# Two-block layer kernel: row numbers for the second experts by a table in memory

## What is computed

```python
g_star = jnp.argmax(p_group, axis=-1)
e_sel = jnp.take_along_axis(e_logits, g_star[:, None, None], axis=1)[:, 0]
top_v, top_i = lax.top_k(softmax(e_sel), 2)
expert_idx = g_star[:, None] * 4 + top_i
...
a = einsum("nd,edf->nef", h, w_gate)      # D=1024, F=256
b = einsum("nd,edf->nef", h, w_up)
u = silu(a) * b * combine[..., None]      # zero but for the two chosen experts
y = einsum("nef,efd->nd", u, w_down)
```

## Time and profile before

| what | us |
|---|---|
| runs | 1757.52, 1756.31, 1753.81 (median 1756.31) |
| profiled execution | 1755.57 |
| its span, first to last instruction | 1753.8 |
| TensorE busy | 1680.8 (96%) |
| VectorE busy | 723.7 (41%) |
| ScalarE busy | 402.5 (23%) |
| GpSimd busy | 21.9 (1%) |

### The profile page before, as it was taken

How to read it: one execution, slowest core, us unless ns; L and a number is a source line. 1 busy time by engine, 2 the same in 40 slices (tenths; PEclk the granted TensorE clock), 3 DMA queues, 4 the chain that set the end, 5 groups by cost and what they waited for, 6 DMA issues and landing times. The chain is left out here.

```text
span 1753.8 us, 21522 instructions
## 1 busy us (share of the span) xinstructions
PE 1680.8 (96%) x8621; PEld 942.0 (54%) x8621; DVE 723.7 (41%) x1333; ACT 402.5 (23%) x742; POOL 21.9 (1%) x29
## 2 busy tenths in 40 slices
PE   7999999999999999999999999999999998987987
PEld 3576565568876443444344334444488664454543
DVE  4645523667545011011101216975762514451515
ACT  5212113443123110101010031116631023311112
POOL 0000000000000000000000000000000000000001
PEclk9999999999999999999999999999999999999999
DMA  9421276111324999999999960311122131279964
GB/s 363 142 93 48 81 260 235 49 49 48 144 97 191 408 419 427 422 419 421 428 419 420 422 248 27 118 48 49 49 96 77 68 144 72 110 295 376 326 253 180
DMA packets 90287, 374.37 MB, mean 213 GB/s; under 512 B 10381, under 2 KB 11741, under 8 KB 75101
## 3 DMA queue, kind: packets, MB, share of 16 engines
q1 hardware_dynamic: 82652, 350.16, 50.7%
q10 hardware_dynamic: 4496, 12.06, 1.8%
q0 software_dynamic: 3056, 11.01, 1.7%
HBM read 466.53 MB, written 10.49 MB: 272 GB/s over the span
## 5 line engine op out<-in xcount | busy, mean ns | idle before, releaser
L2261 PE MATMUL bank<-H,weight_slots 128*128 128x512 f32 (+1 forms) x704 | 280.7, 556 | 0.0
L2261 PEld LDWEIGHTS bank<-H,weight_slots 128*128 128x128 f32 x704 | 133.3, 191 | 143.4 <-issue 139.8
L2697 PE MATMUL bank<-weight_slots,SM 128*64 128x512 f32 x640 | 143.9, 595 | 9.4 <-DMA weight_slots<-in_w_up_e 9.4
L2369 PE MATMUL bank<-R,weight_slots 128*128 128x256 f32 x560 | 124.1, 380 | 0.0
L2369 PEld LDWEIGHTS bank<-R,weight_slots 128*128 128x128 f32 x560 | 105.8, 190 | 16.0 <-issue 1.9
L2727 PE MATMUL bank<-weight_slots,SM 128*64 128x512 f32 x384 | 112.0, 594 | 0.3 <-DMA weight_slots<-in_w_down_e 0.3
L3075 PE MATMUL bank<-weight_slots,SM 128*32 128x256 f32 x1536 | 91.7, 392 | 16.0 <-DMA weight_slots<-in_expert_w_gate 7.8
L2261 PE MATMUL bank<-R 128*128 128x128 f32 (+2 forms) x784 | 101.8, 282 | 4.3 <-ACT R L1193 2.0
L2697 PEld LDWEIGHTS bank<-weight_slots,SM 128*64 128x64 f32 x640 | 45.4, 137 | 104.2 <-issue 84.2
L1787 DVE TENSOR_TENSOR R<-SM,bank 128x512 f32<-128x512 f32 x16 | 11.0, 688 | 217.3 <-PE bank L2697 217.3
L2261 PEld LDWEIGHTS bank<-R 128*128 128x128 f32 x784 | 92.7, 192 | 8.6 <-issue 2.9
(11 more groups left out here) (519 smaller groups left out, 2101.2 us busy)
## 6 DMA issues: line engine op xcount, KB each, us to landing
weight_slots<-in_expert_w_gate SPq DMA_DIRECT2D x51, 1024.0 KB
weight_slots<-in_expert_w_up SPq DMA_DIRECT2D x51, 1024.0 KB
R<-in_expert_w_down SPq DMA_DIRECT2D x51, 1024.0 KB
weight_slots<-in_w_up_e SPq DMA_DIRECT2D x24, 2048.0 KB, 17.3
weight_slots<-in_w_down_e SPq DMA_DIRECT2D x24, 2048.0 KB, 23.6
weight_slots<-in_w_in SPq DMA_DIRECT2D x18, 2048.0 KB, 9.6
weight_slots<-in_w_gate_e SPq DMA_DIRECT2D x16, 2048.0 KB, 17.0
weight_slots<-in_w_ada SPq DMA_DIRECT2D x12, 2048.0 KB, 10.8
```

The source lines that it names most:

```text
L2261: ins = nc.tensor.matmul(dst, lhsT, rhs, start=(i == 0), stop=(i == len(pairs) - 1))
L2369: ins = nc.tensor.matmul(bank_half(name, i, half)[:, TC * tile:TC * (tile + 1)], lhs[:, kk, m:m + 128], rhs[:, kk, :], start=(begins and k ...
L2697: ins = nc.tensor.matmul(b[64 * half:64 * half + 64, :], xs[:, 4 * rows + k, 64 * e:64 * e + 64], w[k][:, 512 * half:512 * half + 512], st ...
```

## The change

The token numbers of steps 2 to 11 no longer come from products. Memory holds a table `id_table` with one number per row place (1536 of them, set to zero at the start by one more POOL DMA). VectorE makes an integer copy of the token numbers (`token_ids`). When `token_slot` is there, POOL scatters the numbers into the table by eight indirect DMAs (two places for each of four tiles of 128 tokens, four bytes each), waits for all, and reads the table back with four DMAs into `row_table`, a tile of 128 rows by 12 steps. This read turns rows and steps, so it moves single numbers of four bytes, 384 in each DMA. Step 1 keeps its product; its gather stands between the fifth and the sixth scatter. `find_rows` and `name_rows` for steps 2 to 11 are gone from VectorE and TensorE. The gather of step q from 2 on waits for the read-back and for the turned rows of step q-2.

```diff
-    ("rank_mm", 1), ("ids_mm", NQUAD - 1), ("late_mm", 2), ("join_mm", 8),
+    ("rank_mm", 1), ("ids_mm", 1), ("late_mm", 2), ("join_mm", 8),
...
+        token_ids = ctx.enter_context(nc.sbuf_tensor("token_ids", [P, TT], I32))
+        row_table = ctx.enter_context(nc.sbuf_tensor("row_table", [P, NQUAD], I32))
+        id_table = nc.dram_tensor("id_table", (P * NQUAD, 1), I32, kind="Internal").ap()
...
-                    act.wait_ge(sem("rows_blank"), 16 * NSLOT)
+                    act.wait_ge(sem("rows_blank"), 16 * (NSLOT + 1))
...
             nc.vector.memset(zero16, 0.0).then_inc(sem("r_zero"), 1)
+            nc.vector.tensor_copy(token_ids[:, :], token_id).then_inc(sem("token_ids"), 1)
             dve.wait_ge(*reached("rl_mm", 1))
...
             x_turned(0)
-            find_rows(2)
             for q in range(NQUAD):
-                if q + 2 < NQUAD:
-                    name_rows(q + 2)
                 if q + 1 < NQUAD:
                     x_turned(q + 1)
                 hidden(q)
-                if q + 3 < NQUAD:
-                    find_rows(q + 3)
...
-            for q in range(1, NQUAD):
-                pool.wait_ge(sem("row_ids"), q)
-                if q == 8:
-                    pool.wait_ge(sem("q_turn_x"), 2)
-                nc.gpsimd.indirect_dma_start(rows_in[q], None, h_rows, bass.IndirectOffsetOnAxis(ap=row_ids[:, q:q + 1], axis=0)).then_inc(sem(f"rows_in{q % 4}"), 16)
+            nc.gpsimd.dma_start(id_table.rearrange("(p q) a -> p (q a)", q=NQUAD), row_table[:, :]).then_inc(sem("rows_blank"), 16)
+
+            def gather_rows(q, ids):
+
+                nc.gpsimd.indirect_dma_start(rows_in[q], None, h_rows, bass.IndirectOffsetOnAxis(ap=ids[:, q:q + 1], axis=0)).then_inc(sem(f"rows_in{q % 4}"), 16)
+
+            pool.wait_ge(sem("rows_blank"), 16 * (NSLOT + 1))
+            pool.wait_ge(sem("token_ids"), 1)
+            for i in range(2 * TT):
+                pool.wait_ge(*reached("token_slots", 1 + i // TT))
+                nc.gpsimd.indirect_dma_start(id_table, bass.IndirectOffsetOnAxis(ap=token_slot[:, i:i + 1], axis=0), token_ids[:, i % TT:i % TT + 1], None).then_inc(sem("ids_out"), 16)
+                if i == TT:
+                    pool.wait_ge(sem("h_written"), 16 * TT)
+                    pool.wait_ge(sem("row_ids"), 1)
+                    gather_rows(1, row_ids)
+            pool.wait_ge(sem("ids_out"), 16 * 2 * TT)
+            for c in range(NSLOT):
+                nc.gpsimd.dma_start(row_table[BLK * c:BLK * (c + 1), :], by_row[c], allow_slow_non_contiguous=True).then_inc(sem("ids_back"), 16)
+            pool.wait_ge(sem("ids_back"), 16 * NSLOT)
+            for q in range(2, NQUAD):
+                pool.wait_ge(sem("q_turn_x"), 2 * (q - 1))
+                gather_rows(q, row_table)
...
                 gate_up(q, 1)
-                if q + 2 < NQUAD:
-                    name_rows(q + 2)
                 if q + 1 < NQUAD:
                     turn_rows(q + 1)
                 if q in (9, 10):
-                    pe.wait_ge(sem("row_ids"), NQUAD - 1)
+                    pe.wait_ge(sem("row_ids"), 1)
```

More of the change, by code:

```diff
@@ L2227, in _ @@
             nc.gpsimd.memset(row_zeros, 0.0).then_inc(sem("zeros_by_pool"), 1)
-            pool.wait_ge(sem("zeros_by_pool"), 2)
+            nc.gpsimd.memset(row_table[:, :], 0).then_inc(sem("zeros_by_pool"), 1)
+            pool.wait_ge(sem("zeros_by_pool"), 3)
             pool.wait_ge(sem("h_ready"), 2 * KD)
             late_part = y_rows.rearrange("(c q r) d -> c (q r) d", c=NSLOT, q=NQUAD)
+            by_row = id_table.rearrange("(c q r) a -> c r (q a)", c=NSLOT, q=NQUAD)
             for c in range(NSLOT):
@@ L2232, in _ @@
                 nc.gpsimd.dma_start(late_part[c, BLK * LATE[0]:BLK * NQUAD, :], row_zeros[0:2 * BLK, :]).then_inc(sem("rows_blank"), 16)
-            pool.wait_ge(sem("rows_blank"), 16 * NSLOT)
-            pool.wait_ge(sem("h_written"), 16 * TT)
-            for q in range(1, NQUAD):
-                pool.wait_ge(sem("row_ids"), q)
-                if q == 8:
-                    pool.wait_ge(sem("q_turn_x"), 2)
-                nc.gpsimd.indirect_dma_start(rows_in[q], None, h_rows, bass.IndirectOffsetOnAxis(ap=row_ids[:, q:q + 1], axis=0)).then_inc(sem(f"rows_in{q % 4}"), 16)
+            nc.gpsimd.dma_start(id_table.rearrange("(p q) a -> p (q a)", q=NQUAD), row_table[:, :]).then_inc(sem("rows_blank"), 16)
```

## The result

| | before | changed |
|---|---|---|
| median of the runs | 1755.93 us (1753.81 to 1757.52) | 1763.76 us (1761.22 to 1768.75, 4 runs) |
| ratio to before, 95% interval | | 1.0037 (1.002 to 1.0054) |
| profiled execution, its span | 1755.57, 1753.8 us | 1768.75, 1766.0 us |
| mean granted clock | 0.991 | 0.987 |

The forecast was 1758.7 us with a range of 1754.5 to 1771. The changed kernel is slower by 7.8 us between these medians, 6.5 us by the ratio. Both intervals lie above 1, and both profiled executions are the slowest of their sets, so the traces show the loss at its largest.

What follows compares the result with a forecast made beforehand. It took the loop of down product, next down load's issue and landing as the bound in the second experts' steps. Terms 0.1 + 1.0 + 0.9 + 1.3 - 0.9 = +2.4 on 1755.57 gave 1758.0, median 1758.7, range 1754.5 to 1771.

Steps and rivals of the forecast that it cites:

- When the table is back: Scatters, then read-backs on POOL: step 2's gather starts at 1565.3 instead of 1557.43 and lands at 1574.7, bounds 1569 and 1580.
- the lower bound of 0.59: POOL's issue of one 384-piece read-back: at least 0.59 us, at most 3.5, with 2.3 taken.
- The late gather: Step 0's down product ends at 1579.4, step 3's gate load follows about 1585.5, queue nearly dry: +1 us, 0 to 4.
- More work for full DMA engines: Stretch at 0.99 DMA share: the table's 1536 pieces, at 9.7 ns each on an engine, add 0.9 us.
- The read-back's own cost: After the scatters: each read-back is one packet per engine, waiting one or two turns, some 1 to 2 us in all.
- The extra gather: Step 4's gather moves ahead of step 2's up weights: 0.52 MB at 401 GB/s, +1.3 us, bounds 0 and 1.3.
- The naming products: Ten products leave TensorE; only the one at 1681.71 counts, a gain of 0.9 us, bounds 0 and 5.5.
- Rival 1: Read-back drains piece by piece beside weights, 31 us; step 2's gather starts at 1588; 1769.5 us, chance 0.26.
- Rival 2: TensorE bounds 1624 to 1664; five naming products and the one at 1681.71 count; about 1751 us, chance 0.12.
- The forecast's own sign: Down products of steps 4 to 6 stay 13 us apart, now waiting more than 1 us for their loads.
- Rival 3: POOL takes more than 3.5 us per 384-piece read-back, step 2's gather lands after 1580; 1764 us, chance 0.07.

Runs made afterwards that it cites:

- e1: Kernel before plus the table's blanking and eight scatters that nothing reads, all naming products kept; 6.1 us slower than before, ratio 1.0035.
- e3: e2 plus four read-backs of a table filled beforehand, issued behind step 0's halves; ratio to before 1.0010, 4.7 us slower than e2.
- e2: Changed kernel without naming, scatters, table or read-back, fixed token numbers for steps 2 to 11; 1753.71 us, ratio to before 0.9983.
- e7: Kernel before, no table, naming products of steps 4 to 11 issued earlier, in TensorE's waits and behind turnings; 1759.78 us, ratio 1.0016.
- e11: The changed kernel measured again without edit, beside other kernels, twelve runs; 1761.46 us, ratio to before 1.0017.
- e8: Changed kernel with places 64 bytes apart, scatters after step 0's row pick, products of steps 2 and 3 kept; 1768.75 us, ratio to before 1.0052.
- e1b: e1 with only the first four scatters, all issued before step 1's gather; 1761.75 us, ratio to before 1.0031.

## Why the prediction was right, and where it was not

The forecast, slower by 2.4 us on the profiled execution, had the sign; the range held the time. That 2.4 lies near the 3.9 us of all runs is in good part luck: the two largest costs that the runs show, of the scatters and of a read-back beside full queues, are not in the sum, and other terms make up for them. Its steps:

- **When the table is back: two errors that cancel.** First scatter 0.85 us after its signal and one each 1.24 us: measured 0.84 and 1.27. The last scatter was to land 4.5 us after its issue. It took 11.1; with a spaced table it takes 4.1 to 4.7, so the term holds for the spaced tables. The four read-backs were to take 9.4 us of GpSimd: they took 2.56, 0.64 each, just over the lower bound of 0.59, so here the cost went by the instruction and not by its pieces. The gather of step 2 came 29.2 us after T (1561.01 - 1531.8); the forecast had 1565.3 - 1535.1 = 30.2.
- **The late gather (+1.0).** SP was to find the queue dry because step 0's down product comes late. It came late by 15.0 us from T, not by 7.4, and because of step 0's and step 1's weights and the lower clock behind each wait, not of the gather.
- **More work for full DMA engines (+0.9).** This is the step that failed: "one costs an engine 0.79 x 3 x 16 / 3911 = 9.7 ns, and 1536 of them 0.9 us of sixteen engines". I priced small pieces by their own occupancy, from loads, and gave the 1024 scattered writes no price at all beyond their landing. What they cost is what others suffer. Pieces of weights took four to eight times as long (1.27 and 2.6 us against 0.31) for four us, the up load's completion came 4.6 us behind its last packet, and the scatters alone made e1 6.1 us slower than before. No row of before shows a write of 4 bytes to memory. I should have bounded its effect on its neighbours, not only its length.
- **The read-back's own cost.** I had it at nothing beyond its 0.9 us. Issued late and beside full queues it costs 4.7 us (e3 against e2), with an 8 us wait that would have made the forecast's gather late. In the first profile of the changed kernel the stall hides it: when the last read-back was issued, the weights under way had landed.
- **The extra gather (+1.3).** The gather of step 4 was issued at 1580.36, ahead of step 2's up half as forecast. Its own price was not measured.
- **The naming products (-0.9, bounds 0 and -5.5).** e2, which has the earlier gathers too, gives -3.0: mis-sized, inside its bounds. The part in the steps after 1624 is small, as said: D0 to D9 is 141.9 before, 140.9 in e2, 141.8 changed. e7 gained nothing by moving them.

The parts measured alone add to 6.1 - 3.0 + 4.7 = 7.8 us, more than the 3.9 of the whole. That the stall and the read-back hide each other is suggested by 1.97 against 8.21 us in the first profile, less by e11, where the read-back waited 5.99.

**The rivals.** Rival 1 forecast a drain piece by piece and the gather at 1588: refuted, 1561.01, and by the packet count. Its time, 1769.5, was nearest to the profiled 1768.75, for another reason. Rival 2 (TensorE the bound after 1624) is refuted by the down products of steps 4 to 6 in the changed kernel:

```profile
1648.44 3.64 PE L3104 MATMUL bank<-R 128*32 128x512 f32 x32
1663.79 3.64 PE L3104 MATMUL bank<-R 128*32 128x512 f32 x32 [0.32 <-DMA R<-in_expert_w_down]
1675.80 3.64 PE L3104 MATMUL bank<-R 128*32 128x512 f32 x32
```

They span 27.4 us, and 26.6 before (1637.17 to 1663.77). In the other seven profiles without these products the same two turns take 25.3 to 27.1 us, never the 24.8 of the rival. The forecast's own sign, waits of more than 1 us for these loads, did not show either. Rival 3 is refuted by 0.64 us per read-back; its 1764 matches the first median by accident.

## What to carry to other kernels

A DMA's price is not only its own time: measure what its neighbours' pieces take beside it, by packets and share of a queue in a window of a few us. When small results are scattered into memory, places 64 bytes apart are the safer choice: a table packed at 4 bytes cut the loads beside it to between a fifth and a ninth of their rate, though the gain in time of spacing it was not clear of noise. And where steps are paced by weights, taking work off TensorE, or keeping its clock up, can show in its rows and hardly in the time.

## What the runs showed of the hardware

- Scattered 4-byte writes into a 6 KB table held 8 KB loads to 31 to 53 GB/s for four us, 0.31 us a piece turning into 1.3 to 2.6, and four of the eight scatters were enough (41 GB/s). With 64 bytes between places: 285 to 309 GB/s.
- A scatter of 128 numbers is 32 packets (160 for five in e8).
- The completion of a weight load came 4.6 us behind its last packet while packed scatters were still open (0.8 us before, and 0.3 in e1b, where the last scatter had been issued 14 us earlier).
- Four read-backs of 1.5 KB in 384 pieces each: 0.64 us each to issue; from the last issue to landing 1.7 to 2.0 us with nearly idle DMA engines, 5.99 and 8.21 us beside weight loads.
- In e8, while GpSimd issued scatters, TensorE's own stream slowed to groups of six, five and three products each 1.4 us, with its weights at hand. The cause is open.
